# Attention per head over 512 queries with the keys on the partitions, in a one-core hybrid encoder block

## What is computed

```python
q = rms_norm(q_down, g) @ w_uq             # 8 heads of 96: 64 plain, 32 rotary
kv = rms_norm(kv_down, g) @ w_ukv          # per head 64 of key, 64 of value
q, k = rope(rms_norm(q)), rope(rms_norm([k_nope, k_rope]))
s = einsum('bqhd,bkhd->bhqk', q, k) * 96 ** -0.5      # per block of 128 queries
s = where(key_chunk <= query_chunk, s, -inf)          # chunks of 64 tokens
attn = softmax(s) @ v
y_a, y_b = attn @ w_o_mla, conv_branch @ w_conv_out
gates = sigmoid(gate_logits + b_gates)
x = x + (gates[:D] * y_a + gates[D:] * y_b) @ w_out   # then a routed expert layer
```

## Time and profile before

| | |
|---|---|
| median of 3 runs | 1237.68 us (1235.8 to 1242.89) |
| the profiled execution | 1234.38 us, of which the span of its profile is 1232.3 us |
| PE busy | 1154.1 us (94%), 5656 matmul instructions |
| PEld, DVE, ACT, POOL busy | 928.8, 800.5, 555.3, 319.4 us |
| mean granted TensorE clock | 0.967 of full |

### The profile page before, as it was taken

The page is one execution under the profiler, slowest core; times in us unless marked ns, Lnnn a source line. Parts: engine busy times, 40 slices in busy tenths (PEclk is TensorE's granted clock), DMA queues, the critical chain, the costliest instruction groups (busy, mean ns, idle before and its releaser), DMA issues.

```text
span 1232.3 us, 16114 instructions
## 1 busy us (share of the span) xinstructions
PE 1154.1 (94%) x5656; PEld 928.8 (75%) x5656; DVE 800.5 (65%) x919; ACT 555.3 (45%) x737; POOL 319.4 (26%) x316
## 2 busy tenths in 40 slices
PE   4999999999978999999899989998999999998895
PEld 3988888887645567777678878888788888786684
DVE  4438999995423555444456634457799999897792
ACT  3532112222443444444422211113788888786782
POOL 4010000000034422220000000002367777654552
...
GB/s 232 1 52 48 39 48 51 51 51 35 43 1 1 1 1 1 1 1 35 1 188 52 1 107 136 121 183 323 274 357 325 302 328 308 312 309 292 324 218 30
DMA packets 96232, 159.71 MB, mean 130 GB/s; under 512 B 11535, under 2 KB 45498, under 8 KB 96186
## 3 DMA queue, kind: packets, MB, share of 16 engines
...
q10 hardware_dynamic: 64, 0.02, 0.0%
...
## 4 chain that ended last, share of the span: by engine, by line
PE 72%; DMA 11%; DVE 6%; ACT 4%; issue 3%; POOL 2%; SPq 0%; ACTq 0%; DVEq 0%; POOLq 0%
PE pb L1308 18%; PE pb L1310 17%; PE pb L1309 17%; DMA wed_raw<-in_w_e_down 7%; PE pb L1425 4%; PE pb L1448 4%; PE pb L1437 2%; PE pb L1357 2%; PE pb L1573 2%; PE pb L1367 2%; DMA wgu_raw<-in_w_e_up 2%; DMA ws_raw<-in_w_conv_out 1%; PE pb L1508 1%; POOL ssh L517 1%; DVE nmax L1057 1%
## 5 line engine op out<-in xcount | busy, mean ns | idle before, releaser
L1243 DVE TENSOR_TENSOR wgu_lo<-wgu_raw,wgu_hi 128x2048 fp32r<-128x2048 f32 x72 | 165.0, 2292 | 35.6 <-ACT wgu_hi L813 31.3
L939 DVE SCALAR_TENSOR_TENSOR cv<-up,dwc,cv 128x1024 f32<-128x1024 f32 x120 | 154.1, 1284 | 3.7
L1308 PE MATMUL pb<-hT_hi,ws_hi 128*128 128x512 f32 x384 | 151.7, 395 | 0.0
L813 ACT ACTIVATE wgu_hi<-wgu_raw 128x2048 fp32r (+1 forms) x72 | 137.9, 1916 | 27.1 <-SPq L432 16.0
L1310 PE MATMUL pb<-hT_hi,ws_lo 128*128 128x512 f32 x384 | 149.5, 389 | 0.0
L1309 PE MATMUL pb<-hT_lo,ws_hi 128*128 128x512 f32 x384 | 149.5, 389 | 0.0
L1308 PE MATMUL pb<-wgu_hi,hgT_hi 128*128 128x512 f32 x288 | 116.9, 406 | 6.6 <-DVE hgT_lo L1247 6.5
L1310 PE MATMUL pb<-wgu_hi,hgT_lo 128*128 128x512 f32 x288 | 113.0, 392 | 0.0
L1309 PE MATMUL pb<-wgu_lo,hgT_hi 128*128 128x512 f32 x288 | 112.3, 390 | 0.0
L516 POOL TENSOR_SCALAR ssh<-ssh 128x8 f32<-128x8 f32 x16 | 3.2, 198 | 403.8 <-DVE ssh L998 402.9
L581 POOL DMA_INDIRECT out<-yb,rcol x36 | 70.7, 1963 | 113.4 <-ACT yb L860 59.8
(11 more groups left out here) (293 smaller groups left out, 2465.7 us busy)
## 6 DMA issues: line engine op xcount, KB each, us to landing
...
wout<-in_w_out SPq DMA_DIRECT2D x1, 4096.0 KB, 12.8
...
```

The lines of the kernel that those rows point to most:

```text
L813: a.activation(wgu_hi[q % 2][:, :, ks, :], raw, ACT.Copy).then_inc(gu_hi, 1)
L939: i = v.scalar_tensor_tensor(out=cv[:, c, :], in0=src, scalar=w, in1=cv[:, c, :], op0=ALU.mult, op1=ALU.add)
L1243: v.tensor_tensor(wgu_lo[q % 2][:, :, ks, :], wgu_raw[:, bass.ds((e + (SLOTS - 1)) % SLOTS, 1), :, ks, :].rearrange("p o g k f -> p (o g) ...
L1308: t_.matmul(out, w(0), m(0), start=start, stop=False)
```

## The change

Attention now goes by items n = 0 to 15: head n % 8 over 512 queries at once (group n // 8). An item is a row of chunks k of 128 keys, 4 for the first eight items and 8 for the others; x numbers all 96 chunks. `scores_T(x)` has the keys on the partitions and up to 512 queries in a row, as three float32r products; the four chunks of an item on the diagonal are 512, 384, 256 and 128 queries wide. The negated maximum of each query is already in the product: k carries four columns of ones behind its 96 and q four rows that hold it. It comes from a pass of its own (`max_scores`, one float32r product per 128 queries with its mask, DVE's maximum behind it, a transpose `mT` of the maxima), made two items ahead; q is transposed three items ahead (`qT`). `exps(x)` writes the probabilities in the layout that the value product wants, and `probs_T` with its copies goes away. In `pv(x)` the 128 loaded weights are a head's 64 values beside 64 columns of ones, so that the sums come out below or above the values; bank 6 holds one item. At an item's end ACT copies the sums and DVE the values, and every second item DVE takes the reciprocal of the sums of a pair of heads and multiplies (`normalise`). k and q are kept in float32r halves, which need the room of the gates: the gates go through a ring of four tiles to DRAM (`gates_d`, 16 transfers issued by ACT) and come back by 16 transfers of SP. Scaling k moved from POOL to DVE. There are two banks for the pieces. The pieces of tile 1 joined those of tile 0 in the last unit, those of tiles 2 and 3 stand in `OPENING` ahead of the first chunk, and those of tiles 4 to 7 in items 0 to 3.

```diff
-    qT = place("qT", [P, 2, HEADS * P], F32, QTO)
-    attnT = place("attnT", [P, 4, T], F32, R3 + 16 * K)
-    kT = place("kT", [P, HEADS, T], F32, R1)
-    vv = place("vv", [P, NTILE, HEADS * VD], F32, R1 + 32 * K)
-    pr = place("pr", [P, 2, T], F32, R1 + 48 * K)
+    gring = place("gring", [P, 4, T], F32, R2)
+    attnT = place("attnT", [P, 2, 4, CW], F32, R3 + 16 * K)
+    kT = [place("kT_hi", [P, HEADS, T], F32R, R1), place("kT_lo", [P, HEADS, T], F32R, R1 + 32 * K)]
+    vv = place("vv", [P, NTILE, HEADS // 2, 3 * VD], F32, R2 + 32 * K)
+    q_at = (QTO, QTO + 4 * K, R2 + 12 * K)
+    qT = [[place(f"qT_{n}{r}", [P, CW], F32R, o + 2 * K * s) for s, n in enumerate(("hi", "lo"))] for r, o in enumerate(q_at)]
+    qn = [place(f"qn{t}", [P, HEADS, QK], F32, o) for t, o in enumerate(
+        (R2 + 56 * K, R6 + 16 * K, R6 + 12 * K, R6 + 20 * K, R2, R2 + 3 * K, R2 + 6 * K, R2 + 9 * K))]
+    kn = [place(f"kn{i}", [P, HEADS, QK + 4], F32, o) for i, o in enumerate((R2 + 59 * K, R2 + 16 * K))]
+    pT = place("pT", [P, 3, CW], F32, R2 + 22 * K + 256)
+    psum_ = place("prob_sums", [P, CW], F32, R2 + 28 * K + 256)
...
+        ITEMS, GT = 2 * HEADS, NTILE // 2
+
+        def chunks(n):
+            return GT * (n // HEADS + 1)
+
+        XOF = [sum(chunks(m) for m in range(n)) for n in range(ITEMS + 1)]
+        XALL = [(n, k) for n in range(ITEMS) for k in range(chunks(n))]
+
+        def col0(n, k):
+            return max(0, k - GT * (n // HEADS)) * P
...
+        UNIT_AT = {(0, 0): ("qdT", 0), (0, 3): ("q0", 0), (0, 4): ("q1", 0), (0, 5): ("kv0", 0), (0, 6): ("kv1", 0), (0, 7): ("qdT", 1),
+                   (1, 2): ("q0", 1), (1, 3): ("q1", 1), (1, 4): ("kv0", 1), (1, 5): ("kv1", 1)}
+        LAST_UNIT = list(UNIT_AT.values())
+
+        def parts(t):
+            return [(kind, t) for kind in ("qdT", "q0", "q1", "kv0", "kv1")]
+
+        def turn(t):
+            return [("kT0", t), ("kT1", t)]
+
+        def maxima(n):
+            return [(f"mx{i}", n) for i in range(GT)]
+
+        OPENING = (turn(0) + parts(2) + turn(1) + parts(3) + turn(2) + turn(3)
+                   + [("qT", 0), ("qT", 1)] + maxima(0) + [("qT", 2)] + maxima(1) + [("mT", 0)])
+
+        def slots(n, k):
+
+            w = []
+            if n < HEADS:
+                w += {0: [("mT", n + 1)], 1: maxima(n + 2)[0:2], 2: maxima(n + 2)[2:4], 3: [("qT", n + 3)]}[k]
+                if n < GT:
+                    w += {0: parts(GT + n)[0:2], 1: parts(GT + n)[2:3], 2: parts(GT + n)[3:4], 3: parts(GT + n)[4:5]}[k]
+                if 1 <= n <= GT and k in (1, 2):
+                    w.append(turn(GT + n - 1)[k - 1])
+            else:
+                w += {1: [("mT", n + 1)], 7: [("qT", n + 3)]}.get(k, maxima(n + 2)[k - 2:k - 1] if 2 <= k <= 5 else [])
+            return [(kind, t) for kind, t in w if t < (ITEMS if kind[0] == "m" or kind == "qT" else NTILE)]
...
+        EARLY = ((ITEMS - 2, 1), (ITEMS - 1, 1))
+        SPLIT_AT = ((ITEMS - 4, 4), (ITEMS - 3, 4), (ITEMS - 2, 4))
...
+            def gate_back(c):
+                if c == KD - 1:
+                    sp.wait_ge(att_ok, HEADS)
+                for half in range(2):
+                    sp.dma_start(gates[:, half * KD + c, :], gates_d[half * KD + c]).then_inc(gate_in[c], 16)
...
+                    for i in range(4):
+                        sp.wait_ge(gate_out[i], 16 * 4)
+                    sp.wait_ge(pv_ok, len(XALL))
+                    gate_back(0)
+                    gate_back(1)
+                if c == 2:
                     sp.wait_ge(sp_hi, 4)
                     sp.wait_ge(sp_lo, 4)
                     sp.dma_start(wout[:, :, :], w_out[0].rearrange("(k p) c -> p k c", p=P)).then_inc(wout_in, 16)
+                if 2 <= c < 5:
+                    gate_back(2 * c - 2)
+                    gate_back(2 * c - 1)
...
-                    a.activation(gates[:, c, :], src, ACT.Sigmoid, bias=vcol[:, V_BG + c:V_BG + c + 1]).then_inc(u_ev, 1)
+                    if c >= 4:
+                        act.wait_ge(gate_out[c % 4], 16 * (c // 4))
+                    a.activation(gring[:, c % 4, :], src, ACT.Sigmoid, bias=vcol[:, V_BG + c:V_BG + c + 1]).then_inc(u_ev, 1)
+                    act.wait_ge(u_ev, u + 1)
+                    act.dma_start(gates_d[c], gring[:, c % 4, :]).then_inc(gate_out[c % 4], 16)
...
+            def exps(x):
+                n, k = XALL[x]
+                c0 = col0(n, k)
+                act.wait_ge(sT_ok, x + 1)
+                if x >= 3:
+                    act.wait_ge(pv_ok, x - 2)
+                a.activation(pT[:, x % 3, c0:CW], pb[:, 4 + x % 2, c0:CW], ACT.Exp).then_inc(ex_ok, 1)
...
+                if k + 1 == chunks(n):
+                    h = n % HEADS
+                    act.wait_ge(pv_ok, XOF[n + 1])
+                    if n >= 2:
+                        act.wait_ge(att_ok, n // 2)
+                    a.activation(psum_[v_rows(h), :], pb[sum_rows(h), 6, :], ACT.Copy).then_inc(sum_ok, 1)
...
+                if kind[:2] == "mx":
+                    y = GT * t + int(kind[2])
+                    w = (GT * (t // HEADS) + int(kind[2]) + 1) * P
+                    dve.wait_ge(sc_ok, y + 1)
+                    v.tensor_reduce(out=nmax[t % 2][:, QK + y % GT:QK + y % GT + 1], in_=banks(2 * (y % 2), 2)[:, 0:w],
+                                    axis=AX.X, op=ALU.max, negate=True).then_inc(mx_ok, 1)
+                    return
...
+                    if kind == "kT0":
+                        k = kn[t % 2]
+                        if t == 0:
+                            dve.wait_ge(tab_ok, 1)
+                        dve.wait_ge(head_rs, t + 1)
+                        v.tensor_tensor(k[:, :, 0:NOPE], k[:, :, 0:NOPE], s2[:, 1, :].unsqueeze(2).broadcast_to([P, HEADS, NOPE]), ALU.mult)
+                        v.tensor_tensor(k[:, :, NOPE:QK], krr[:, t:t + 1, :].broadcast_to([P, HEADS, ROPE]),
+                                        s2[:, 1, :].unsqueeze(2).broadcast_to([P, HEADS, ROPE]), ALU.mult).then_inc(k_ok, 1)
+                    dve.wait_ge(qk_hi, hi_of[kind, t] + 1)
+                    cols = slice(t * P, (t + 1) * P)
+                    v.scalar_tensor_tensor(out=kT[1][0:QK, h:h + 4, cols], in0=M[0:QK, :].rearrange("p (h t) -> p h t", h=4),
+                                           scalar=vcol[0:QK, V_NK:V_NK + 1], in1=kT[0][0:QK, h:h + 4, cols].bitcast(F32),
+                                           op0=ALU.mult, op1=ALU.subtract).then_inc(m_free[b], 1)
+                if kind == "qT":
+                    dve.wait_ge(qk_hi, hi_of[kind, t] + 1)
+                    hi, lo = qT[t % 3]
+                    v.scalar_tensor_tensor(out=lo[0:QK, :], in0=M[0:QK, :], scalar=vcol[0:QK, V_NQ:V_NQ + 1], in1=hi[0:QK, :].bitcast(F32),
+                                           op0=ALU.mult, op1=ALU.subtract).then_inc(m_free[b], 1)
+                if kind == "mT":
+                    rows = slice(QK, QK + 4)
+                    dve.wait_ge(m_full[b], nth + 1)
+                    v.tensor_tensor(qT[t % 3][0][rows, :].rearrange("p (i t) -> p i t", i=GT), M[rows, 0:P].unsqueeze(1).broadcast_to([4, GT, P]),
+                                    own_tile[rows, :, :], ALU.mult).then_inc(m_free[b], 1)
...
+            def normalise(pair):
+
+                dve.wait_ge(sum_ok, 2 * pair + 2)
+                dve.wait_ge(val_ok, 2 * pair + 2)
+                o = attnT[:, pair // 4, pair % 4, :]
+                link(v.reciprocal(psum_[:, :], psum_[:, :]))
+                v.tensor_tensor(o, o, psum_[:, :], ALU.mult).then_inc(att_ok, 1)
...
+            for m, k in XALL:
+                for kind, t in slots(m, k):
+                    misc(kind, t)
+                if (m, k) in EARLY:
+                    unit_lo(IN_UNITS + EARLY.index((m, k)))
+                if m % 2 == 0 and m >= 2 and k == chunks(m) - (1 if m < HEADS else 5):
+                    normalise(m // 2 - 1)
+                if (m, k) in SPLIT_AT:
+                    split_lo(SPLIT_AT.index((m, k)))
+                if k + 1 == chunks(m):
+                    h = m % HEADS
+                    dve.wait_ge(pv_ok, XOF[m + 1])
+                    v.tensor_copy(attnT[v_rows(h), m // HEADS, h // 2, :], pb[v_rows(h), 6, :]).then_inc(val_ok, 1)
+            normalise(HEADS - 1)
+            split_lo(3)
...
+            def max_scores(n, i):
+
+                j, h, y = GT * (n // HEADS) + i, n % HEADS, GT * n + i
+                w = (j + 1) * P
+                pe.wait_ge(qk_hi, hi_of["qT", n] + 1)
+                if y >= 2:
+                    pe.wait_ge(mx_ok, y - 1)
+                if n == HEADS and i == 0:
+                    pe.wait_ge(m_free[1], used[1])
+                S = banks(2 * (y % 2), 2)
+                for f in range(0, w, 512):
+                    e = min(w, f + 512)
+                    t_.matmul(S[:, f:e], qT[n % 3][0][0:QK, i * P:(i + 1) * P], kT[0][0:QK, h, f:e], start=True, stop=(e < w))
```

(50 more changed lines are left out.)

348 lines of the change are left out of this document (145 added, 203 removed).

## The result

The changed kernel takes 1321.2 us (median of 4 runs, 1317.5 to 1322.3) against 1236.7, a ratio of 1.0682, 95% interval 1.0649 to 1.0714. I had forecast 1287 with a range of 1244 to 1308. The direction is right, the size is short by 34 us, and the time lies 13 us above the range.

A forecast was written before the change was run, and what follows sets the result against it. PE was taken as the bound, busy 94% of the span. From the profiled 1234.4 us, +26 for work and holes, +29 clock and -1 stage end gave 1288; forecast 1287, range 1244 to 1308.

The forecast's parts named there:

- The end of the stage: Where attention hands over to the branches: hole of 2.6 us, gates' transfers hidden, in total -1 us.
- The holes: PE waiting at hand-overs in the attention stage: pieces' chain, scaling of k, reciprocal, copy of the values at item boundaries.
- The forecast's schedule without the clock: Last unit +6, opening 46, items 0-3 77, items 4-7 46, items 8-15 118: 293 against 267, +26 us.
- 205 us, 21 less than before: PE's own work in the attention stage after the change, summed from single product prices, against 226 us before.
- the 7 us of narrow products: Bound on PE's work: 128-column float32r products priced at 0.11 us each; at float32's rate, 0.23, 7 us more.
- the clock, 29: Lower granted clock after holes in the attention stage costs PE 29 us, bounds 0 and 45.
- 2.2 per hole: Clock loss in us behind each new hole of 3.5 us and more, six in items 1-3, two at reciprocals: 18.
- 0.11 for 52 columns: Trace price in us of a 52-column float32r product, called twice its columns' rate and taken for 128 columns.
- A (faster): Rival: PE's holes in attention stay at 41 us, stage 246, 1213 us; decides at 62 us holes and clock; chance 0.13.
- B: Rival: the walk of attention's holes is right but PE stays at 2.4 GHz, 1259 us; chance 0.22.
- C, the forecast: Holes and low clock in the attention stage together, 1270 to 1305 us; chance 0.47.
- D: Rival: 128-column float32r products at float32's rate, or gates arriving late, 7 to 15 more, 1300 or more; chance 0.13.

The follow-up runs named there:

- With the clock held: Changed kernel with idle products (results unread) put into PE's holes, the second version with more of them: 1279.8 us, ratio 1.0340.
- the kernel with all three edits: Changed kernel with reordered pieces and early reciprocal, work moved to item boundaries, and idle products in PE's holes: 1248.3 us, ratio 1.0101.
- 35 us for the order: Changed kernel with the pieces in another order, DVE's sums and k's scaling as steps of their own: 1285.8 us, ratio 1.0357.
- 15 for the reciprocal: Changed kernel with the reciprocal and its product behind chunk 1 instead of chunk 3 in items 2, 4 and 6: 1306.0 us, ratio 1.0545.
- 13.5 for the boundaries: Kernel with reordered pieces and early reciprocal, plus `qT` and one maximum moved behind an item's last value product: 1260.0 us, ratio 1.0185.
- the kernel with both edits: Changed kernel with the pieces in another order and the reciprocal earlier: 1273.5 us, ratio 1.0277.
- with idle products: Kernel with reordered pieces and early reciprocal, plus idle products in the holes left in the opening and items 0 to 7: 1255.7 us, ratio 1.0166.

## Why the prediction was right in direction and short in size

*Where the time goes.* Right. The loss is in the attention stage and, with 7.3 (forecast 6), in the last unit. The end of the stage was forecast at -1 and is 616.7 against 617.9. PE's hole ahead of the attention half is 2.5 (forecast 2.6). The gates' transfers stay hidden: a 512 KB piece lands in 9.7 us, and what ACT waits for ws_raw, 15.5 in two waits, answers to the 18.7 of the earlier trace rows.

*The holes.* Right by kind, near in size. The forecast's schedule without the clock was 287 us from the last unit on, of which 200 PE's work, so 87 of standing still. With the clock held it is 309, of which 225 work, so 84 (225 is measured in the kernel with all three edits). `kn`, `qdT` and `attnT` lead PE's waits, and the edits that move each of them take it away (35 us for the order, 15 for the reciprocal, 13.5 for the boundaries, each with the clock that came with it). A full chunk takes 1.6, as forecast.

*The failed step: "205 us, 21 less than before".* PE's work is 225 behind the last unit, with tile 1's 4.9 in it 230; before it was 226 by my count, and the 245.4 busy us at a clock of 0.93 are about the same. The gain on which all else was set off isn't there. I had priced every product by its distance from a neighbour of its own kind, 0.22 and 0.91 in even streams and 0.15 for the mask. The change doubles the number of masks to 128 and puts them between float32r and float32 products. The 64 of the maxima cost 0.33 each, 0.18 more than counted, 11 us in all; the 64 of the scores cost 0.10 more each in a full chunk, 6 us. That is 17 or 18 of the 25 that are missing. Where the other 7 lie is not shown; a part can be that busy time holds the recorded length of the last product ahead of each hole, which is longer than its price. The step made the sum too small by about 22 (309 against 287), and the only bound that I had given it was the 7 us of narrow products.

*The mis-sized term: the clock, 29.* It measured 40 to 41. The rows from which I took 2.2 per hole showed PE dense for a long time behind its hole. In items 1 and 2 the clock was low for less than 4 us behind each hole, which can have cost no more than my 2.2. But it was at 0.50 from 388 to 419, and from 525 to 583 with PE busy 49.0 of 58.0 us, with the end of a hole of 5.3 and one of 4.3 in it. A fixed price per hole doesn't describe that; the upper bound of 45 held. The Trainium skill (TensorE: Matmul & The Clock Gate, section "A second HAM failure mode: psum-queue depth-cycling") says that a PE that stands still briefly and often between groups of products swings between its two clocks, and pays in throughput though each product alone looks normal. The traces agree that short standing still can cost the clock: in the kernel with both edits it was 0.50 from 500 to 532 with no hole over 0.7, and with idle products nearly everywhere 1.00. They show it staying low there, not swinging.

The two together are 22 + 11 = 33. By the spans of the profiled executions the kernels are 88.1 apart where I had 54, so 34 are missing. (My sum started from the profiled execution's 1234.4, while the median before is 1236.7; from there it would have given 1291.) One reading of mine was wrong without touching the sum: 0.11 for 52 columns is five times, not twice, what they take by the rate of the earlier trace rows; twice is true of the 128 columns that I priced with it, and those did measure 0.11.

*The rivals.* A (faster) was out: its 62 us of holes and low clock were over 120. B's walk gives 1259; with the clock held it is 1279.8, the difference being PE's work. C, the forecast, had both parts of its mechanism, holes and low clock, but its range ended at 1305. D's range held the time, but not by its mechanism: narrow products are at 0.11, and the gates come in time.

*What stays open.* What brings the clock back. At 1.00 the holes of 1.4 at the boundaries of items 8 to 13 left it there; at 0.50, with holes no longer, it stayed low for 32 us and more. Idle products settle it from outside, but the rows don't say which condition decides. And why a mask slows its neighbours.
